# Two hybrid layers: gate and merge as one stage, the post norm by chunk, scale vectors loaded ahead

## The chip, the core and the metric

The kernel runs on one core of one Trainium2 chip. TensorE does the matrix products and the 128x128 turns (transposes), VectorE, ScalarE and GpSimd the elementwise work, SyncE (SP) issues most transfers. The metric is the device time of one execution in microseconds (us), the median of several.

## The reference, cut to what matters

The reference computes two transformer blocks with mixers and experts, and behind them two hybrid layers. The change lies in the hybrid layers alone:

```python
def hybrid_layer(x, p_i, ...):
    h = rmsnorm(x, g_pre)
    proj = h @ w_in                       # four mixers' inputs, gate paths, 4 x 1024 merge logits
    o = stack([o_a, o_b, o_c, o_d])       # sparse attention, short conv, stick-breaking attention, spatial gating
    o = o * silu(gate_paths)
    z = einsum('bsnw,nwd->bsnd', o, w_branch)
    g = sigmoid(merge_logits + b_merge)
    merged = sum(g * z, axis=2)
    y = merged @ w_out
    x = x + rmsnorm(y, g_post)
    x = x + (p_i @ w_ple) * sigmoid(x @ w_ple_gate)
    return x
```

There are 512 tokens of width 1024, everything in float32. `rmsnorm(x, g)` is `x * rsqrt(mean(x*x) + 1e-6) * g`.

## The kernel before, in words

The program is a list of stages. Each stage has one function for each engine, and the functions write out, in order, what that engine issues; nothing reorders it. A wait stands for a semaphore value, and `fence(P, e, stage)` waits until all four compute engines have reached the end of a stage. The 512 tokens are four chunks `c` of 128 rows. The eight PSUM banks are handed out in turn, and a bank is taken again when its last content has been read. Weights pass through a ring of four 2 MB slots; SP fetches the next weights as soon as the slot's user has freed it, in one fixed order.

A hybrid layer has the stages `h_norm`, `h_mix`, `h_attend`, `h_gate`, `h_merge` and `h_out`, and in `hybrid` they follow each other twice (l = 0 and 1). What each does:

- `h_norm` squares each chunk on ScalarE, forms the reciprocal root for two chunks at a time on GpSimd (`pool_rstd`: a multiply-add and a power), multiplies on VectorE with the scale vector `gpre` (a broadcast DMA that GpSimd issues), and turns h on TensorE.
- `h_gate` multiplies o by silu on VectorE and turns it into oT: TensorE turns half a chunk into a bank, and VectorE (half 0) or ScalarE (half 1) copies it out.
- `h_merge` computes the merge logits in two fp32r parts. `hp` holds hT split into a high and a low part, `wp` the same for a half (`part(p)`) of the weights: ScalarE writes the high part, VectorE three quarters of the low part and GpSimd the last quarter. There are eight quarters q of two halves each; for each q, TensorE does 2 x 96 instructions into four banks, and then four branch products (`c,oT`), one for each chunk. `place` on VectorE and ScalarE handles one chunk: add the bias, sigmoid, times the branch product, sum. The tile of the gate, `sg`, has two buffers, so the chunks take turns.
- `h_out` turns the merged rows mg, multiplies by w_out (`kept('wo')`, two column halves n of four chunks c, each copied out by ScalarE), multiplies p by w_ple, normalizes y (`norm_act` on ScalarE, `pool_rstd` on GpSimd, two instructions a chunk on VectorE), turns the new x, and multiplies by w_ple_gate.

In the profile a helper's line stands for all of its users: L62 is a product, L66 a turn, L72 an activation, L75, L81, L87 are VectorE's or GpSimd's two-input, three-input and copy instructions, L78 a multiply-add, L117 a DMA. So the names of the tiles tell the stages apart: `wp,hp` is the merge's product, `c,oT` a branch or output product, `ident,mg`, `ident,mx` and `ident,h` are the turns of the merged rows, of x (`mx`) and of h.

Of the kernel before, what the change touches and what calls it, by code (L numbers as in the profile page):

```python
# [11 lines left out]
ACT = mybir.ActivationFunctionType  # L12
# [2910 lines left out]
def hybrid(P, I, x, cs, dst, ring, front, ready):  # L2923
    for l in range(2):
        k_ = lambda *a, l=l: (f'h{l}',) + a
        with ExitStack() as c:
            oT = P.sb([128, 8, 512], name="oT", ctx=c)
            hT = P.sb([128, 8, 512], name="hT", ctx=c)
            h_norm(P, I, l, k_, x, hT, front, ready)
            with ExitStack() as d:  # L2930
                o = P.sb([128, 4, D], name="o", ctx=d)
                aV = P.sb([128, 4, 256], name="aV", ctx=d)
                qkT = P.sb([128, 4, 512], name="qkT", ctx=d)
                iT = P.sb([128, 2, 512], name="iT", ctx=d)
                big = P.sb([128, 10, 512], name="big", ctx=d)
                fc = P.sb([128, 4, 512], name="fc", ctx=d)
                tok = P.sb([128, 4, 768], name="tok", ctx=d)
                madd = x[:, 4:6].rearrange("p a (b n) -> p (a b) n", b=2)
                h_mix(P, I, l, k_, ring, cs, hT, o, aV, qkT, iT, big, fc, tok, madd)
                silu = h_attend(P, I, l, k_, ring, hT, oT, o, aV, qkT, big, fc, tok, madd)  # L2940
                h_gate(P, k_, o, oT, silu)
            mg = P.sb([128, 4, D], name="mg", ctx=c)
            h_merge(P, I, l, k_, ring, hT, oT, mg, x[:, 4:6])
            h_out(P, I, l, k_, ring, oT, mg, hT, x)
        front = k_('out')
        ready = lambda c, k_=k_: P.dve.at(*k_('xout', 4 + c))
    h_store(P, dst, x, front, ready)
# [46 lines left out]
def h_norm(P, I, l, k_, x, hT, front, ready):  # L2994
# [3 lines left out]
    g = P.sb([128, D], name="gpre", ctx=d)  # L2998
# [27 lines left out]
    def dve(e):  # L3026
        fence(P, e, front)
        e.wait_ge(*s_g.at(*k_('g')))
        for c in G4:
            e.wait_ge(*P.pool.at(*k_('rs', c // 2)))  # L3030
            e.scalar_tensor_tensor(out=h[:, c, :], in0=x[:, c, :], scalar=rs[:, c:c + 1], in1=g[:], op0=MUL, op1=MUL).then_inc(*P.dve.inc(*k_('normed', c)))
# [550 lines left out]
def h_gate(P, k_, o, oT, silu):  # L3582
    def pe(e):
        fence(P, e, k_('attend'))
        for c in G4:
            for half in range(2):
                e.wait_ge(*P.dve.at(*k_('gated', half, c)))
                pe_turns(P, e, k_('oT', c, half), [o[:, c, (4 * half + j) * 128:(4 * half + j + 1) * 128] for j in range(4)],
                         (P.act if half else P.dve,) + k_('oT', c, half))
        P.end(k_('gate'), P.pe)  # L3590

    def dst(c, half):
        return oT[:, half * 4:half * 4 + 4, c * 128:(c + 1) * 128], P.bank(*k_('oT', c, half)).rearrange("p (j n) -> p j n", j=4)

    def act(e):
        fence(P, e, k_('attend'))
        for c in G4:
            e.wait_ge(*P.pe.at(*k_('oT', c, 1)))
            e.activation(*dst(c, 1), ACT.Copy).then_inc(*P.act.inc(*k_('oT', c, 1)))
        P.end(k_('gate'), P.act)  # L3600

    def dve(e):
        fence(P, e, k_('attend'))

        def gate(c):
            for n in range(2):
                ov = o[:, c, n * 512:n * 512 + 512]
                e.scalar_tensor_tensor(out=ov, in0=ov, scalar=0.5, in1=silu[:, 2 * c + n], op0=MUL, op1=MUL).then_inc(*P.dve.inc(*k_('gated', n, c)))

        gate(0)  # L3610
        for c in G4:
            if c < 3:
                gate(c + 1)
            e.wait_ge(*P.pe.at(*k_('oT', c, 0)))
            e.tensor_copy(*dst(c, 0)).then_inc(*P.dve.inc(*k_('oT', c, 0)))
        P.end(k_('gate'), P.dve)

    def pool(e):
        fence(P, e, k_('attend'))
        P.end(k_('gate'), P.pool)  # L3620

    P.stage(pe, act, dve, pool, nothing)


def h_merge(P, I, l, k_, ring, hT, oT, mg, spare):
    d = ExitStack()
    sg, bm = (spare[:, i].rearrange("p (a n) -> p a n", a=2) for i in range(2))
# [11 lines left out]
    def in_order(part, half, place):  # L3639
        part(0)  # L3640
# [11 lines left out]

    def pe(e):
        fence(P, e, k_('gate'))
# [23 lines left out]
        def place(n, q, i):  # L3678
# [13 lines left out]
    def act(e):  # L3692
        fence(P, e, k_('gate'))
        for h in range(2):
            e.activation(hp[:, 0, 4 * h:4 * h + 4], hT[:, 4 * h:4 * h + 4], ACT.Copy).then_inc(*P.act.inc(*k_('hhigh', h)))

# [6 lines left out]
        def place(n, q, i):  # L3703
            e.wait_ge(*P.dve.at(*k_('biased', n)))
            e.activation(sg[:, n % 2, :], sg[:, n % 2, :], ACT.Sigmoid).then_inc(*P.act.inc(*k_('sig', n)))

        in_order(part, skip, place)
        P.end(k_('merge'), P.act)

    def dve(e):  # L3710
        fence(P, e, k_('gate'))
        for h in range(2):
# [7 lines left out]
        def place(n, q, i):  # L3720
            S, mv = sg[:, n % 2, :], mg[:, i, (q % 2) * 512:(q % 2) * 512 + 512]
# [14 lines left out]

        in_order(part, skip, place)
        P.end(k_('merge'), P.dve)

    def pool(e):  # L3740
        fence(P, e, k_('gate'))
# [11 lines left out]

        in_order(part, half, skip)
# [13 lines left out]
def h_out(P, I, l, k_, ring, mT, y, xT, x):  # L3768
# [38 lines left out]
    def act(e):  # L3807
# [19 lines left out]
        norm_act(P, e, k_('post'), y, junk[:], ss, G4)  # L3827
# [10 lines left out]
    def dve(e):  # L3838
# [25 lines left out]
    def pool(e):  # L3864
# [3 lines left out]
        e.wait_ge(*P.act.at(k_('post'), 'square', 3))  # L3868
        pool_rstd(P, e, rs[:, 0:4], ss[:, 0:4], D, EPS, *k_('post'))
# [28 lines left out]
def program(nc, I, out):  # L3898
    with ExitStack() as ctx:
# [20 lines left out]
        with ExitStack() as c:  # L3920
            ring = Ring(P, 4, "c", c)
            hybrid(P, I, x, cs, out[0], ring, ('moe1', 'experts'), lambda c: P.dve.at('moe1', 'result', c))
# [28 lines left out]
```

## Time and profile before

| what | value |
|---|---|
| time, median of 3 runs | 4548.87 us (4538.51 to 4552.62) |
| the profiled execution's own time | 4555.35 us |
| its span | 4553.6 us |
| mean granted TensorE clock | 0.915 |
| TensorE busy | 4006.0 us, 88% |
| VectorE, ScalarE, GpSimd busy | 1662.4, 1133.3, 414.7 us |

Busy time is summed over the span; TensorE's clock is given as a share of 2.4 GHz, and 0.5 of it is 1.2 GHz. The hybrid layers take the stretch from about 3102 us to the end. Layer 0 has its merge at 3435 to 3671 us and layer 1 at 4156 to 4391 us.

### The profile page before, as it was taken

What the parts mean: (1) busy time and instruction counts of PE and PEld (TensorE: products, weight loads), DVE (VectorE), ACT (ScalarE), POOL (GpSimd) and SP (SyncE); (2) the same over time, 40 slices, a digit from 0 to 9 for tenths busy, and PEclk for the clock granted to TensorE, in tenths of its full rate; (3) what the DMA queues carried; (4) which work ended last, traced back from release to release, by engine and by line L of the source; (5) the groups of instructions that cost most, each with busy time, mean ns of one, the idle gap of its engine ahead of it and who ended that gap; (6) DMA issues with size and microseconds to landing.
All of it is one profiled execution on the core that took longest, in us unless ns stands there. A gap on an engine that the chain in (4) does not pass through costs nothing.

```text
span 4553.6 us, 58245 instructions
## 1 busy us (share of the span) xinstructions
PE 4006.0 (88%) x25387; PEld 2336.4 (51%) x25387; DVE 1662.4 (37%) x2920; ACT 1133.3 (25%) x2163; POOL 414.7 (9%) x430
## 2 busy tenths in 40 slices
PE   7998888999999966468999798888988988988997
PEld 4546645333335424368898432224556744455753
DVE  2205531122233027755544412224643313644322
ACT  2114411111123137633343110001142211133211
POOL 2200020000000012301001100000002200001200
PEclk9999998999999977656797899999999999989999
DMA  6341034988873139733341399994103212112221
GB/s 233 111 146 33 17 121 159 370 324 326 327 274 132 43 110 297 232 111 103 91 124 50 153 384 409 409 409 180 46 1 135 99 63 79 39 37 93 102 83 37
DMA packets 358670, 739.05 MB, mean 162 GB/s; under 512 B 67184, under 2 KB 143456, under 8 KB 358416
## 3 DMA queue, kind: packets, MB, share of 16 engines
q1 hardware_dynamic: 348416, 697.93, 42.2%
q0 software_dynamic: 10000, 37.41, 2.3%
q8 instruction: 199, 3.26, 0.3%
q14 instruction: 55, 0.45, 0.0%
HBM read 673.39 MB, written 61.89 MB: 161 GB/s over the span
## 4 chain that ended last, share of the span: by engine, by line
PE 75%; DMA 9%; DVE 9%; ACT 5%; issue 1%; SPq 1%; POOL 0%; DVEq 0%; POOLq 0%; ACTq 0%
PE ps L62 72%; DMA raw<-in_moe_w_dram 6%; PE ps L66 3%; DVE mx L75 1%; ACT naS L72 1%; DMA b<-in_ada_w_dram 1%; SPq L117 1%; DVE nast L90 1%; DVE o L75 1%; DMA a<-in_ada_w_dram 0%; DVE ps L75 0%; ACT b L72 0%; ACT c L72 0%; DVE b L75 0%; DVE spr L75 0%
## 5 line engine op out<-in xcount | busy, mean ns | idle before, releaser
L62 PE MATMUL ps<-raw,xinT 128*64 128x512 f32 (+1 forms) x4096 | 595.9, 493 | 54.1 <-DMA raw<-in_moe_w_dram 45.4
L62 PE MATMUL ps<-c,hT 128*128 128x512 f32 (+2 forms) x1024 | 420.6, 565 | 5.7 <-ACT hT L72 3.5
L62 PEld LDWEIGHTS ps<-raw,xinT 128*64 128x64 f32 (+1 forms) x4096 | 194.5, 123 | 436.0 <-issue 286.2
L62 PE MATMUL ps<-wp,hp 128*128 128x512 f32 x1536 | 360.3, 396 | 20.2 <-DVE wp L75 20.2
L62 PE MATMUL ps<-a,nahT 128*128 128x512 f32 x768 | 338.2, 597 | 5.6 <-ACT nahT L72 5.2
L62 PEld LDWEIGHTS ps<-wp,hp 128*128 128x128 f32 x1536 | 290.9, 190 | 87.0 <-issue 27.0
L62 PEld LDWEIGHTS ps<-c,hT 128*128 128x128 f32 x1024 | 192.6, 193 | 201.0 <-issue 194.2
L62 PE MATMUL ps<-raw,hidT 128*64 128x512 f32 x1024 | 240.0, 604 | 16.5 <-DMA raw<-in_moe_w_dram 16.2
L62 PEld LDWEIGHTS ps<-a,nahT 128*128 128x128 f32 x768 | 144.2, 191 | 178.6 <-issue 178.0
L62 PE MATMUL ps<-c,oT 128*128 128x512 f32 x512 | 222.8, 593 | 1.4 <-ACT oT L72 1.4
L75 DVE TENSOR_TENSOR mx<-mx,ps 128x512 f32<-128x512 f32 (+1 forms) x164 | 106.6, 661 | 219.5 <-PE ps L62 184.7
L62 PEld LDWEIGHTS ps<-c,oT 128*128 128x128 f32 x512 | 97.0, 190 | 116.9 <-issue 111.0
L62 PE MATMUL ps<-xr,b 128*128 128x512 f32 (+1 forms) x384 | 143.9, 535 | 7.6 <-DVE xr L81 7.5
L62 PEld LDWEIGHTS ps<-raw,hidT 128*64 128x64 f32 x1024 | 67.2, 137 | 148.6 <-issue 113.5
L62 PE MATMUL ps<-hT,c 128*128 128x512 f32 x320 | 142.5, 606 | 0.0
L75 DVE TENSOR_TENSOR wp<-c,wp 128x1536 fp32r<-128x1536 f32 x32 | 60.4, 1892 | 221.6 <-ACT wp L72 221.6
L72 ACT ACTIVATE hidT<-ps 128x512 f32<-128x512 f32 x32 | 19.1, 597 | 453.4 <-PE ps L66 453.4
L75 DVE TENSOR_TENSOR hid<-hid,ps 128x512 f32<-128x512 f32 x64 | 44.0, 687 | 240.6 <-ACT hid L72 217.6
L75 POOL TENSOR_TENSOR wp<-c,wp 128x512 fp32r<-128x512 f32 x32 | 89.1, 2786 | 353.5 <-ACT wp L72 353.5
L81 DVE SCALAR_TENSOR_TENSOR xr<-xx,pv,xr 128x768 f32<-128x768 f32 x48 | 45.7, 1015 | 206.1 <-ACT xr L72 205.8
L72 ACT ACTIVATE wp<-c 128x2048 fp32r<-128x2048 f32 x32 | 60.9, 1910 | 217.0 <-PE ps L62 217.0
L62 PEld LDWEIGHTS ps<-xr,b 128*128 128x128 f32 x384 | 73.5, 194 | 77.4 <-issue 61.9
(456 smaller groups left out, 5866.8 us busy)
## 6 DMA issues: line engine op xcount, KB each, us to landing
raw<-in_moe_w_dram SPq DMA_DIRECT2D x384, 1024.0 KB, 9.6
c<-in_w_in_dram SPq DMA_DIRECT2D x28, 2048.0 KB, 9.1
a<-in_ada_w_dram SPq DMA_DIRECT2D x16, 2048.0 KB, 12.9
b<-in_ada_w_dram SPq DMA_DIRECT2D x8, 2048.0 KB, 10.5
a<-in_na_w_qkv_dram SPq DMA_DIRECT2D x6, 2048.0 KB, 19.0
c<-in_w_branch_dram SPq DMA_DIRECT2D x16, 512.0 KB, 4.2
c<-in_w_out_dram SPq DMA_DIRECT2D x4, 2048.0 KB, 9.1
c<-in_w_ple_gate_dram SPq DMA_DIRECT2D x4, 2048.0 KB, 7.8
```

What stands on the lines that cost most here:

```text
L62: return self.e.matmul(out, lhsT, rhs, start=start, stop=stop, skip_group_check=True) if self.e is not None else self
L66: return self.e.transpose(out, in_, ident[0:k, 0:k]) if self.e is not None else self
L72: return self.e.activation(*a, **k) if self.e is not None else self
L75: return self.e.tensor_tensor(*a, **k) if self.e is not None else self
L81: return self.e.scalar_tensor_tensor(**k) if self.e is not None else self
L90: return self.e.tensor_reduce(*a, **k) if self.e is not None else self
L117: return self.e.dma_start(*a) if self.e is not None else self
```

## The change

- `h_gate` and `h_merge` become one stage, so one fence falls away. In it ScalarE's order is: split half of hT, high part of the first weights, one turned tile, the other half of hT, three turned tiles. The first split (`low(0)`), the first low part and the second split follow VectorE's gate work.
- The gate tile `sg` has four buffers, one for each chunk, in the spare part of x (`x[:, 4:6]`), and the bias `bm` has a tile of its own. VectorE adds the bias for all four chunks of a quarter first, then does the rest chunk by chunk.
- In `h_out` the square of chunk c is issued right behind the copy of y's second half for that chunk, inside `kept('wo')`, and the reciprocal root is formed for each chunk.
- In `h_norm` the scale vector lies in `x[:, 4]`, and its load is issued behind the merge stage (layer 1) or behind the routing of the second expert stage (layer 0). The reciprocal root is formed for each chunk.

On ScalarE, at the start of the merge of layer 0 (`hp` is hT split, `wp<-c` the high part of weights, `oT<-ps` a turned tile copied out):

```order
 L72 ACTIVATE o<-ps 128x256 x2
-L72 ACTIVATE oT<-ps 128x4x128 x4
-L72 ACTIVATE hp<-hT 128x2048 x2
-L72 ACTIVATE wp<-c 128x2048 x4
+L72 ACTIVATE hp<-hT 128x2048
+L72 ACTIVATE wp<-c 128x2048
+L72 ACTIVATE oT<-ps 128x4x128
+L72 ACTIVATE hp<-hT 128x2048
+L72 ACTIVATE oT<-ps 128x4x128 x3
+L72 ACTIVATE wp<-c 128x2048 x3
 L72 ACT_TABLE_LOAD
```

The splits of hT and the first high part moved ahead of the turned tiles; the number of instructions is the same.

On ScalarE, in the output stage of layer 0 (`mg<-ps` is a copy of y, `ojunk,oss` a square with its sum, `pT` and `ple` the tiles of p):

```order
-L72 ACTIVATE mg<-ps 128x512 x8
+L72 ACTIVATE mg<-ps 128x512 x5
+L72 ACTIVATE ojunk,oss<-mg 128x1024
+L72 ACTIVATE mg<-ps 128x512
+L72 ACTIVATE ojunk,oss<-mg 128x1024
+L72 ACTIVATE mg<-ps 128x512
+L72 ACTIVATE ojunk,oss<-mg 128x1024
+L72 ACTIVATE mg<-ps 128x512
+L72 ACTIVATE ojunk,oss<-mg 128x1024
 L72 ACTIVATE pT<-ps 128x512 x2
 L72 ACTIVATE ple<-ps 128x512 x8
-L72 ACTIVATE ojunk,oss<-mg 128x1024 x4
```

The four squares moved from behind the ple copies to between the copies of y, and the last of them stands ahead of the two copies of pT.

On VectorE, in the last quarter of the merge of layer 0, before (`mx` is the gate tile, `mg` the merged rows):

```order
L75 TENSOR_TENSOR mx<-ps,mx 128x512
L75 TENSOR_TENSOR mx<-mx,ps 128x512
L75 TENSOR_TENSOR mg<-mg,mx 128x512
L75 TENSOR_TENSOR mx<-ps,mx 128x512
L75 TENSOR_TENSOR mx<-mx,ps 128x512
L75 TENSOR_TENSOR mg<-mg,mx 128x512
L87 COPY oT<-ps 128x4x128 x4
```

and now:

```order
L75 TENSOR_TENSOR mx<-ps,bm 128x512 x4
L75 TENSOR_TENSOR mx<-mx,ps 128x512
L75 TENSOR_TENSOR mg<-mg,mx 128x512
L75 TENSOR_TENSOR mx<-mx,ps 128x512
L75 TENSOR_TENSOR mg<-mg,mx 128x512
L75 TENSOR_TENSOR mx<-mx,ps 128x512
L75 TENSOR_TENSOR mg<-mg,mx 128x512
L75 TENSOR_TENSOR mx<-mx,ps 128x512
L75 TENSOR_TENSOR mg<-mg,mx 128x512
L87 COPY oT<-ps 128x4x128 x4
```

The first excerpt shows the last two of four chunks; the adds of all four now stand together at the front.

The diff, cut to its core:

```diff
@@ h_norm
-    g = P.sb([128, D], name="gpre", ctx=d)
+    g = x[:, 4, :]
...
+        fence(P, e, spare)
+        e.dma_start(g, bc(I['g_pre_2'][l])).then_inc(*s_g.inc(*k_('g')))
         fence(P, e, front)
-        e.dma_start(g[:], bc(I['g_pre_2'][l])).then_inc(*s_g.inc(*k_('g')))
-        for i in range(2):
-            e.wait_ge(*P.act.at(k_('norm'), 'square', 2 * i + 1))
-            pool_rstd(P, e, rs[:, 2 * i:2 * i + 2], ss[:, 2 * i:2 * i + 2], D, EPS, *k_('rs', i))
+        for c in G4:
+            e.wait_ge(*P.act.at(k_('norm'), 'square', c))
+            pool_rstd(P, e, rs[:, c:c + 1], ss[:, c:c + 1], D, EPS, *k_('rs', c))
@@ h_merge, ScalarE
-        fence(P, e, k_('gate'))
-        for h in range(2):
+        fence(P, e, k_('attend'))
+        def high(h):
             e.activation(hp[:, 0, 4 * h:4 * h + 4], hT[:, 4 * h:4 * h + 4], ACT.Copy).then_inc(*P.act.inc(*k_('hhigh', h)))
...
+        high(0)
+        part(0)
+        turn(0)
+        high(1)
+        for c in (1, 2, 3):
+            turn(c)
         in_order(part, skip, place)
@@ h_merge, VectorE
-            e.wait_ge(*P.pe.at(*k_('merge', 2 * q + 1, i, 'half')))
-            e.wait_ge(*s_b[q % 2].at(*k_('bm', q)))
-            if n >= 2:
-                e.wait_ge(*P.dve.at(*k_('merged', n - 2)))
-            e.tensor_tensor(S, P.bank(*k_('merge', q, i)), bm[:, q % 2, :], ADD).then_inc(*P.dve.inc(*k_('biased', n)))
+            for j in G4 if i == 0 else ():
+                e.wait_ge(*P.pe.at(*k_('merge', 2 * q + 1, j, 'half')))
+                e.wait_ge(*s_b[q % 2].at(*k_('bm', q)))
+                if q:
+                    e.wait_ge(*P.dve.at(*k_('merged', n + j - 4)))
+                e.tensor_tensor(sg[:, j, :], P.bank(*k_('merge', q, j)), bm[:, q % 2, :], ADD).then_inc(*P.dve.inc(*k_('biased', n + j)))
+            if n == 0:
+                e.wait_ge(*P.pe.at(*k_('oT', 3, 1)))
...
+        gate(0)
+        for c in G4:
+            if c < 3:
+                gate(c + 1)
+            e.wait_ge(*P.pe.at(*k_('oT', c, 0)))
+            e.tensor_copy(*turned(c, 0)).then_inc(*P.dve.inc(*k_('oT', c, 0)))
+        low(0)
+        part(0)
+        low(1)
         in_order(part, skip, place)
@@ h_out
+                    if what == 'wo' and n == 1:
+                        e.wait_ge(*P.act.last())
+                        e.activation(junk[:], y[:, c, :], ACT.Square, accum_out=ss[:, c:c + 1]).then_inc(*P.act.inc(*k_('post', 'square', c)))
...
-        norm_act(P, e, k_('post'), y, junk[:], ss, G4)
...
-        e.wait_ge(*P.act.at(k_('post'), 'square', 3))
-        pool_rstd(P, e, rs[:, 0:4], ss[:, 0:4], D, EPS, *k_('post'))
+        for c in G4:
+            e.wait_ge(*P.act.at(*k_('post', 'square', c)))
+            pool_rstd(P, e, rs[:, c:c + 1], ss[:, c:c + 1], D, EPS, *k_('post', c))
```

## Rows read from the trace of the kernel before

**Rows 1.** The page: the span, and TensorE's busy time.
```profile
span 4553.6 us, 58245 instructions
...
PE 4006.0 (88%) x25387; PEld 2336.4 (51%) x25387; DVE 1662.4 (37%) x2920; ACT 1133.3 (25%) x2163; POOL 414.7 (9%) x430
```

**Rows 2.** Waits, 3380 us on: who waited for whom; us in total, times, longest.
```profile
PE ps L66 <- DVE mx L75: 21.9, 8, 9.5
...
PE ps L62 <- DVE wp L75: 20.2, 2, 10.1
...
PE ps L66 <- DVE h L81: 9.7, 1, 9.7
...
PE ps L66 <- DVE mg L75: 9.6, 2, 4.8
```

**Rows 3.** Chain of waits through layer 0: start us, us, what.
```profile
3425.86 1.92 ACT hp L72
...
3427.91 4.49 DVE hp L75 x2
3432.40 2.76 DVE wp L75
...
3435.29 226.02 PE ps L62 x884
```

**Rows 4.** DMA issues, 3418.3 to 3419 us: KB each, us to landing.
```profile
c<-in_w_in_dram SPq DMA_DIRECT2D x1, 2048.0 KB, 8.9
```

**Rows 5.** Timeline, start of merge: start, us, engine, line, what [idle before <-releaser].
```profile
3418.32 0.37 SPq L117 DMA_DIRECT2D c<-in_w_in_dram  x1
...
3450.27 1.76 DVE L75 TENSOR_TENSOR wp<-c,wp 128x1536 fp32r<-128x1536 f32 x1 [12.38 <-ACT wp L72]
3450.33 2.85 POOL L75 TENSOR_TENSOR wp<-c,wp 128x512 fp32r<-128x512 f32 x1 [13.48 <-ACT wp L72]
```

**Rows 6.** Timeline, last quarter of layer 0's merge.
```profile
3659.42 7.03 PE L62 MATMUL ps<-c,oT 128*128 128x512 f32 x16
...
3661.34 0.69 DVE L75 TENSOR_TENSOR mx<-mx,ps 128x512 f32<-128x512 f32 x1 [9.19 <-PE ps L62]
...
3663.39 0.63 ACT L72 ACTIVATE mx<-mx 128x512 f32<-128x512 f32 x1 [10.57 <-DVE mx L75]
...
3670.40 0.69 DVE L75 TENSOR_TENSOR mg<-mg,mx 128x512 f32<-128x512 f32 x1
```

**Rows 7.** Timeline, output stage of layer 0.
```profile
3732.31 1.04 PE L66 MATMUL ps<-ident,pp 128*128 128x128 f32 x8
...
3734.14 14.00 PE L62 MATMUL ps<-c,pT 128*128 128x512 f32 x32 [0.79 <-ACT pT L72]
...
3748.80 1.06 ACT L72 ACTIVATE ojunk<-mg 128x1024 f32<-128x1024 f32 x1
...
3767.64 7.56 PE L62 MATMUL ps<-c,hT 128*128 128x512 f32 x17 [0.69 <-ACT hT L72]
```

**Rows 8.** Windows, turns of mg and x: us, busy (count), PEclk, DMA share, GB/s.
```profile
3671.20:3677.20 6.00, 5.34 (x32) 5.14 (x32) 2.77 (x4) 2.37 (x4) 1.30 (x2) 0.72 0.55 175
3757.60:3767.20 9.60, 7.87 (x32) 6.28 (x32) 9.50 (x10) 2.00 (x4) 0.00 (x0) 0.52 0.00 0
```

**Rows 9.** Timeline, norm of layer 1.
```profile
3823.54 10.51 SPq L117 DMA_DIRECT2D c<-in_w_in_dram  x4
...
3831.11 4.87 DVE L81 SCALAR_TENSOR_TENSOR h<-mx,hrs,gpre 128x1024 f32<-128x1024 f32 x4 [6.19 <-DMA gpre<-in_g_pre_dram]
...
3839.86 2.38 PE L62 MATMUL ps<-c,hT 128*128 128x512 f32 x5 [0.73 <-ACT hT L72]
```

**Rows 10.** Timeline, norm of layer 0: VectorE's first pair, GpSimd's second power.
```profile
3109.68 2.48 DVE L81 SCALAR_TENSOR_TENSOR h<-mx,hrs,gpre 128x1024 f32<-128x1024 f32 x2
...
3111.10 1.62 POOL L75 TENSOR_TENSOR hrs<-hrs,mhalf 128x2 f32<-128x2 f32 x1
```

**Rows 11.** Tile hrs: GpSimd's powers in the norms; ns min/median/max.
```profile
L75 POOL TENSOR_TENSOR hrs<-hrs,mhalf x4: 688/726/1620, 3108.0 to 3828.7; 128x2 f32<-128x2 f32 x4
```

More of the change, by code:

```diff
@@ L2920, with hybrid @@
 G4 = range(4)
-def hybrid(P, I, x, cs, dst, ring, front, ready):
+def hybrid(P, I, x, cs, dst, ring, front, spare, ready):
     for l in range(2):
@@ L2940, in hybrid @@
                 silu = h_attend(P, I, l, k_, ring, hT, oT, o, aV, qkT, big, fc, tok, madd)
[L2941 removed]
             mg = P.sb([128, 4, D], name="mg", ctx=c)
[L2943 removed]
+            h_merge(P, I, l, k_, ring, hT, o, oT, silu, mg, x[:, 4:6])
             h_out(P, I, l, k_, ring, oT, mg, hT, x)
[L2945 removed]
+        front, spare = k_('out'), k_('merge')
         ready = lambda c, k_=k_: P.dve.at(*k_('xout', 4 + c))
@@ L3579, in h_attend, with h_merge @@
     return silu
[L3582 to L3625, printed above, removed]
+def h_merge(P, I, l, k_, ring, hT, o, oT, silu, mg, spare):
     d = ExitStack()
-    sg, bm = (spare[:, i].rearrange("p (a n) -> p a n", a=2) for i in range(2))
+    sg = spare.rearrange("p a (b n) -> p (a b) n", b=2)
+    bm = P.sb([128, 2, 512], name="bm", ctx=d)
     hp = P.sb([128, 2, 8, 512], F32R, name="hp", ctx=d)
@@ L3651, in skip, with turned @@
         pass
+    def turned(c, half):
+        return oT[:, half * 4:half * 4 + 4, c * 128:(c + 1) * 128], P.bank(*k_('oT', c, half)).rearrange("p (j n) -> p j n", j=4)
     def pe(e):
-        fence(P, e, k_('gate'))
+        fence(P, e, k_('attend'))
+        for c in G4:
+            for half in range(2):
+                e.wait_ge(*P.dve.at(*k_('gated', half, c)))
+                pe_turns(P, e, k_('oT', c, half), [o[:, c, (4 * half + j) * 128:(4 * half + j + 1) * 128] for j in range(4)],
+                         (P.act if half else P.dve,) + k_('oT', c, half))
         def half(q, h):
@@ L3692, in act, with turn @@
     def act(e):
-        fence(P, e, k_('gate'))
-        for h in range(2):
+        fence(P, e, k_('attend'))
+        def high(h):
             e.activation(hp[:, 0, 4 * h:4 * h + 4], hT[:, 4 * h:4 * h + 4], ACT.Copy).then_inc(*P.act.inc(*k_('hhigh', h)))
+        def turn(c):
+            e.wait_ge(*P.pe.at(*k_('oT', c, 1)))
+            e.activation(*turned(c, 1), ACT.Copy).then_inc(*P.act.inc(*k_('oT', c, 1)))
         def part(p):
@@ L3710, in dve, with gate, low @@
     def dve(e):
-        fence(P, e, k_('gate'))
-        for h in range(2):
+        fence(P, e, k_('attend'))
+        def gate(c):
+            for n in range(2):
+                ov = o[:, c, n * 512:n * 512 + 512]
+                e.scalar_tensor_tensor(out=ov, in0=ov, scalar=0.5, in1=silu[:, 2 * c + n], op0=MUL, op1=MUL).then_inc(*P.dve.inc(*k_('gated', n, c)))
+        def low(h):
             e.wait_ge(*P.act.at(*k_('hhigh', h)))
@@ L3740, in pool @@
     def pool(e):
-        fence(P, e, k_('gate'))
+        fence(P, e, k_('attend'))
         def part(p):
@@ L3752, in half @@
                 e.dma_start(bm[:, q % 2, :], bc(I['b_merge_2'][l, c0:c0 + 512])).then_inc(*s_b[q % 2].inc(*k_('bm', q)))
+        part(0)
         in_order(part, half, skip)
@@ L3921, in program @@
             ring = Ring(P, 4, "c", c)
-            hybrid(P, I, x, cs, out[0], ring, ('moe1', 'experts'), lambda c: P.dve.at('moe1', 'result', c))
+            hybrid(P, I, x, cs, out[0], ring, ('moe1', 'experts'), ('moe1', 'route'), lambda c: P.dve.at('moe1', 'result', c))
         P.emit()
```

19 lines of the change are left out of this document (11 added, 8 removed).

## The prediction

> **What bounds the kernel now.** I read the page first, then the table of waits of the hybrid layers (the stretch from 3380 us on), then the chain of waits through layer 0 of them, and last the timelines around every hole in TensorE's row. TensorE is busy for 88% of the span [rows 1]; a change that touches no matmul can only win the holes in its row. In the hybrid layers the table of waits names four of them that the diff touches: before the merge's first product (10.1 us, twice), before the turns of the merged rows (4.8, twice), before the turns of the new x (9.5 and three times 0.5, twice), and before the turns of the normed rows of layer 1 (9.7, once) [rows 2]. Inside the eight quarters of a merge TensorE never waits: the chain has one piece of 226 us of products there [rows 3]. So what the diff does inside a quarter is worth nothing as long as that stays so, and the forecast is what becomes of the four holes.
>
> The sum is made against the profiled execution (4555.35 us, span 4553.6); the median of the three timed runs, 4548.87, lies 6.5 below it and the gain is taken off that. Times below are places in the profile of before, layer 0; layer 1 repeats them. From no change this measurement can tell about 0.3%, 13.6 us.
>
> **A. Start of the merge.** Now ScalarE finishes the last turned tile at 3425.8, splits hT in two pieces until 3429.6, VectorE answers with 4.49 us for the low halves and 2.76 for the first weights' low part, and TensorE starts at 3435.29 [rows 3]. The change issues the same instructions, earlier: ScalarE's first split of hT can start when attention ends (3418.4) and VectorE's `low(0)` follows its last gate copy at 3425.7, at 2.25 (half of 4.49), so to 3427.95. ScalarE's next instruction, `part(0)`, waits for the weights. Their transfer is issued at 3418.32, when attention frees the ring's slot, and lands 8.9 us later [rows 4, 5]: 3427.2. The change doesn't move that. Queued behind this wait on ScalarE are `turn(0)`, the second split of hT, `turn(1)` to `turn(3)` and `part(1)`; TensorE's turns don't wait for them, since eight turned tiles fill eight banks. So: 3427.3 + 1.92 (ScalarE, as for the equally wide split of hT) = 3429.2, + 1.76 on VectorE [rows 5] + waits = 3431.1, TensorE at 3431.2 instead of 3435.3. Its second half, wanted 12 us later, gets `high(1)` at 3435.3 and its low part at 3437.2, in time. The clock falls in both cases: TensorE's turns end at 3425.2 (10.09 before its start [rows 2]) and 6.0 us of idleness are left, where 4.8 us were followed by turns at half clock (below). I take **4.1 a layer, 8.2**. Bounds: no gain if those weights land 4 us later; at most 4.3, since they can't be used before they land.
>
> For VectorE's 1.76: in the steady quarters VectorE and GpSimd start together on their shares of a part, VectorE 0.06 earlier, with 1.76 and 2.85 us [rows 5]; in the first one of before, GpSimd was ahead and VectorE needed 2.76 [rows 3]. In the new order both wait for the same ScalarE instruction, so I take 1.76. The other order would cost 1.0 a layer.
>
> **B. End of the merge.** In the last quarter VectorE waits 9.19 us for the first branch product, then does bias add, (ScalarE's sigmoid,) product, sum for each tile in turn; the last product of TensorE ends at 3666.45 and VectorE's last sum only at 3671.1 [rows 6]. With four gate tiles the four adds and sigmoids are done before the first branch product is there: the fourth half product ends at 3659.4, its add (0.69) and sigmoid (0.63) by 3661.0. What is left behind a branch product is a product and a sum, 1.4 us, less than the 1.76 between two branch products (7.03 for four). The last ends at 3666.6 + 1.4 = 3668.0, and the turns start at 3668.15 instead of 3671.24: 3.1 us. The turns themselves take 5.34 us at a mean clock of 0.72 [rows 8], where eight warm ones take 1.04, so 32 take 4.2 [rows 7]; with 1.7 us of idleness in place of 4.8 the clock may hold. I take half of that 1.1: **3.6 a layer, 7.2** (bounds 3.1 and 4.2).
>
> **C. Post norm.** Now the four squares (1.06 us, one each 1.18) follow the copies of the ple product, then GpSimd's scale, then VectorE's two instructions a chunk pace the turns, and TensorE, done at 3748.14, starts the gate product at 3767.64 [rows 7]. In the change the square of chunk c follows its second copy. TensorE takes 0.44 us for an instruction (14.00 for 32 [rows 7]) and 16 of them for such a chunk, 7.0, so squares 0 to 2, their scales and the updates of x lie beside the output product. Square 3 stands ahead of the two copies of pT on ScalarE, which TensorE waits for: the ple product starts 1.3 us later (1.18 and the wait for the copy) and ends at 3749.4. From the last square (3753.5 now) to the first turn (3757.6) it is 4.1 today, so the fourth square, done at 3734.4, has its update by 3738.5: 11 us early. The turns run at once: 4.2 warm [rows 7] and 0.7 for the last copy, gate product at 3754.3. Gain **13.3 a layer, 26.6**. If the turns stay at half clock (7.87 for 32 [rows 8]), it is 9.6.
>
> **D. Norm of layer 1.** Now VectorE waits 6.2 us for the scale vector, which GpSimd issues only when layer 0 is over; it starts at 3831.1, and the projections start at 3839.86 [rows 9]. Preloaded, into a part of x that the merge leaves free, it is long there: its issue stands behind scale 3 at 3736, on an idle GpSimd. Next in line is GpSimd's scale of each chunk, and here the row of layer 0 speaks: with VectorE in its normalizing instruction GpSimd's power took 1.62 us where the median of four is 0.73, and ended 0.56 after VectorE's second instruction did [rows 10, 11]. Four single scales now alternate with four instructions of 1.28 (4.87 for four, overlapped). The first starts at about 3826.0 (layer 0's end, 3823.54, a square of 1.18, GpSimd's 0.3 + 0.73, waits), then each chunk 1.28 + 0.56 + 0.1 later, the last starting at about 3831.9 and done at 3833.2; four copies of 0.62 follow, projections at 3835.9. Gain **3.9**. The first weights, issued at 3823.54 [rows 9] at the same event as now, land at 3832.5 by the 8.9 of [rows 4], and so don't bound it; they are the upper bound, 7.3. Without that blocking: h done at 3830.9, start at 3833.7, gain 6.2.
>
> The Trainium skill (SBUF — State Buffer, "Who interferes with whom") has the rule for it: a Vector instruction with two SBUF inputs and a GpSimd one that reads SBUF exclude each other, and the second waits for the whole of the first. The trace agrees with 1.62 against 0.73. It speaks against splitting the scale by chunk; by the rule the sum is as here, without it 4500.
>
> **E. Norm of layer 0.** There the scale vector was in time already. VectorE's four instructions came in two pairs; with single scales the third and the fourth each wait: the fourth starts at about 3114.7 instead of 3114.0. **Loss 0.8** (between a loss of 1.5 and a gain of 0.6, if scale 3 slips in ahead).
>
> Sum: 8.2 + 7.2 + 26.6 + 3.9 - 0.8 = 45.1, so 4510.3 for a profiled execution and 4503.8 for the median.
>
> **At no cost.** The gate stage's fence goes; its work starts at the same moment. `bm` in a tile of its own changes an address. Inside a quarter VectorE now does four adds, then four products (and sums), 12 x 0.69 = 8.3 us; TensorE's products of the next quarter want only its adds, which come earlier than now. ScalarE's functions keep their order of kinds, so no table is loaded more. More small instructions on GpSimd lie in its idle time, but for D and E. The matmuls are the same in number and order.
>
> **Rivals.**
> R1, no blocking in the norms (D 6.2, E a gain of 0.6): 4500. Against it stands the 1.62.
> R2, the cheap end: the clock stays low over the turns (C 9.6, B 3.1) and the merge's first weights land too late for A: 0 + 6.2 + 19.2 + 3.9 - 0.8 = 28.5, 4520. For it: turns of x at clock 0.52 [rows 8]; against it: they followed 9.5 us of idleness that goes.
> R3, the change doesn't do what it says: the time comes back as waits for weights, since SP's loads start with fences that the change doesn't move. It needs landings 3 us (D) or, for the first half of w_ple_gate, tens of us later than now; no change, 4540 to 4549.
> R4, slower: the quarters lose their cover. VectorE's block of 8.3 us begins only when its parts are done and holds up the next parts, on which TensorE's halves wait. Now the next part can't start before TensorE has finished the half after (11.2 us into the next quarter, 18 after the branches begin), while the block ends 12 after they begin, and a part is wanted 6 us after it can be done: 12 us a quarter before the first is lost. From 4.2 us lost in each of 14 quarters the kernel is slower by over 0.3%; at 4.5 it would be at 4567. The single piece of 226 us [rows 3] speaks against.
>
> **How the numbers follow.** Forecast 0.67, R1 0.13, R2 0.13, R3 0.05, R4 0.02. The three first are faster by over 0.3%: 0.93; same 0.05; slower 0.02. Range: all terms at their best give 4498, at their worst 4522; the three runs of before lie 14 us apart, so the lower end goes 12 further: 4486 to 4522.
>
> **What would show it.** Merge: TensorE idle 6.0 before its first half, with ScalarE's `part(0)` ended by the DMA; 1.7 before the mg turns. Out: no idleness between ple product and turns, turns of x in 4.2 to 5.3, pT's wait 2.1. Layer 1 norm: no DMA wait, GpSimd's powers at 1.1 to 1.7 us, and 13 us in all from gate product to projections. Wrong is the forecast if a quarter takes more than 28.64 us, or if ScalarE's wait for weights lasts past 3429.

## The result and the profile after

| what | before | after |
|---|---|---|
| median of four runs on one chip | 4550.74 us (4538.51 to 4560.48) | 4498.98 us (4494.41 to 4503.99) |
| the profiled execution's own time | 4555.35 us | 4494.41 us |
| its span | 4553.6 us | 4492.6 us |
| mean granted clock | 0.915 | 0.923 |

The ratio of the times is 0.9888, with a 95% interval of 0.9860 to 0.9915: faster by 51.8 us; the interval reaches from 38.7 to 63.7 us, so the times alone don't tell the forecast of 45.1 from rival R1 (48.8), and the rows below have to. The page of the kernel after, against [rows 1]:

```profile
span 4492.6 us, 58286 instructions
PE 3980.7 (89%) x25387; PEld 2313.7 (52%) x25387; DVE 1655.2 (37%) x2920; ACT 1131.0 (25%) x2163; POOL 428.0 (10%) x450
```

TensorE has the same 25387 instructions. The two profiled spans lie 61.0 us apart, and 9.2 of them have nothing to do with the change: the last product ahead of the hybrid layers (`hl`) ends at 3108.71 us before and at 3099.48 after, in code that is the same but for the early load of layer 0's scale vector (in the kernels of this study it ends anywhere from 3084.95 to 3108.71). So every comparison below starts at that product and ends at the start of the last gate product (`w_ple_gate`). That stretch fell from 1379.16 to 1327.37 us, by 51.8. That this is the timed difference too is chance: it holds 2.7 us of stretches that the change doesn't touch. Cut at TensorE's own instructions it divides like this (us, layer 0 and layer 1):

| stretch on TensorE | before | after |
|---|---|---|
| norm of layer 0, to the projections | 9.14 | 10.00 |
| projections, mixers and attention (not touched) | 307.35 / 305.67 | 305.04 / 305.31 |
| idle before the merge's first half | 10.09 / 10.09 | 5.78 / 5.70 |
| the first half | 23.65 / 23.60 | 24.04 / 24.06 |
| from its end to the last branch product | 207.51 / 207.51 | 207.50 / 207.50 |
| wait and turns of the merged rows | 10.82 / 10.79 | 5.97 / 5.97 |
| output product to gate product | 90.37 / 90.35 | 76.22 / 76.22 |
| gate product of layer 0 and norm of layer 1 | 72.22 | 68.06 |

The waits of the stretch from 3090 us on, next to [rows 2] (columns: us in all, times, longest):

```profile
PE ps L62 <- DVE wp L75: 11.5, 2, 5.8
ACT wp L72 <- DMA c<-in_w_in_dram: 13.9, 2, 7.0
PE ps L66 <- DVE h L81: 7.1, 5, 4.4
```

The hole before the merge is 5.8 us instead of 10.1. The row of the DMA says what bounds it now: ScalarE stands 7.0 us, twice, before the first weights. The waits for `mx`, which were the largest item, are gone.

Start of the merge of layer 0, timeline (columns: start, us, engine, line, operation; in brackets the idle time before it and what ended it), against [rows 3 to 5]:

```profile
3407.64 0.37 SPq L117 DMA_DIRECT2D c<-in_w_in_dram  x1
...
3407.65 1.92 ACT L72 ACTIVATE hp<-hT 128x2048 fp32r<-128x2048 f32 x1
...
3414.92 2.28 DVE L75 TENSOR_TENSOR hp<-hT,hp 128x2048 fp32r<-128x2048 f32 x1
...
3416.55 1.91 ACT L72 ACTIVATE wp<-c 128x2048 fp32r<-128x2048 f32 x1 [6.99 <-DMA c<-in_w_in_dram]
...
3418.49 1.76 DVE L75 TENSOR_TENSOR wp<-c,wp 128x1536 fp32r<-128x1536 f32 x1 [1.29 <-ACT wp L72]
...
3420.30 24.19 PE L62 MATMUL ps<-wp,hp 128*128 128x512 f32 x96 [5.79 <-DVE wp L75]
```

The weights are asked for at 3407.64 and are there at 3416.5, 8.9 later; then 1.91 on ScalarE and 1.76 on VectorE follow one another with hardly a gap, and TensorE starts. This is the forecast chain, with the forecast durations.

End of the merge, against [rows 6]:

```profile
3645.02 0.69 DVE L75 TENSOR_TENSOR mx<-ps,bm 128x512 f32<-128x512 f32 x1 [2.03 <-PE ps L62]
...
3646.73 0.69 DVE L75 TENSOR_TENSOR mx<-mx,ps 128x512 f32<-128x512 f32 x1 [1.02 <-PE ps L62]
...
3652.61 0.69 DVE L75 TENSOR_TENSOR mg<-mg,mx 128x512 f32<-128x512 f32 x1
3653.44 3.69 PE L66 MATMUL ps<-ident,mg 128*128 128x128 f32 x32 [1.60 <-DVE mg L75]
```

VectorE's last sum ends at 3653.30, and TensorE has waited 1.60 instead of 4.79. Its 32 turns take 3.69 instead of 5.34, and the window over them shows a granted clock of 1.00, where [rows 8] had 0.72 (columns: stretch and its length, busy us and instructions of PE, PEld, DVE, ACT, POOL, then the granted clock, DMA share, GB/s):

```profile
3420.30:3444.30 24.00, 24.00 (x96) 19.67 (x97) 6.28 (x3) 5.62 (x6) 7.38 (x4) 0.91 0.46 152
3653.40:3657.10 3.70, 3.66 (x32) 3.48 (x32) 2.45 (x4) 1.79 (x3) 1.30 (x2) 1.00 0.79 226
3729.70:3733.40 3.70, 3.65 (x33) 3.41 (x31) 2.53 (x4) 2.41 (x5) 0.00 (x0) 1.00 0.00 0
```

The first row is the merge's first half, behind its 5.8 us of idleness and still partly at half clock (1.2 GHz; mean 0.91); the second is the turns of the merged rows, the third those of the new x, which had 0.52 in [rows 8]. In the output stage, against [rows 7]:

```profile
3713.68 1.06 ACT L72 ACTIVATE ojunk<-mg 128x1024 f32<-128x1024 f32 x1
3714.74 1.06 ACT L72 ACTIVATE pT<-ps 128x512 f32<-128x512 f32 x2
3715.85 14.00 PE L62 MATMUL ps<-c,pT 128*128 128x512 f32 x32 [1.97 <-ACT pT L72]
...
3717.09 1.23 DVE L75 TENSOR_TENSOR mx<-mx,mg 128x1024 f32<-128x1024 f32 x1
...
3729.69 3.66 PE L66 MATMUL ps<-ident,mx 128*128 128x128 f32 x32
...
3734.03 3.27 PE L62 MATMUL ps<-c,hT 128*128 128x512 f32 x7 [0.69 <-ACT hT L72]
```

The fourth square ends ahead of pT's copies, the last update of x starts at 3717.09, and the turns at 3729.69 follow the ple product with no bracket, which means with no wait.

Norm of layer 1, against [rows 9]:

```profile
3791.25 0.18 POOL L78 TENSOR_SCALAR hrs<-hss 128x1 f32<-128x1 f32 x1 [74.95 <-ACT hjunk L72]
...
3792.20 1.28 DVE L81 SCALAR_TENSOR_TENSOR h<-mx,hrs 128x1024 f32<-128x1024 f32 x1 [0.88 <-POOL hrs L75]
3792.32 1.22 POOL L78 TENSOR_SCALAR hrs<-hss 128x1 f32<-128x1 f32 x1 [0.25 <-ACT hjunk L72]
...
3794.20 1.28 DVE L81 SCALAR_TENSOR_TENSOR h<-mx,hrs 128x1024 f32<-128x1024 f32 x1 [0.72 <-POOL hrs L75]
3794.25 1.28 POOL L78 TENSOR_SCALAR hrs<-hss 128x1 f32<-128x1 f32 x1
3795.62 0.55 POOL L75 TENSOR_TENSOR hrs<-hrs,mhalf 128x1 f32<-128x1 f32 x1
```

No DMA ends a wait here any more. A new one stands in its place: VectorE and GpSimd alternate. GpSimd's multiply-add on 128 numbers takes 0.18 alone and 1.22 to 1.28 where VectorE has started its 1.28 us instruction just ahead of it, and VectorE then waits 0.72 for the scale of the next chunk. VectorE's instructions start 2.0 apart; the four took 4.87 in one piece before. From the end of the gate product to the projections it is 12.9 us, where the prediction named 13.

### The profile page after: what moved, and what is told of

Its sections match the earlier page's. It is cut to its first block, busy times and chain, and to the rows that moved or that the text cites. A ratio compares the mean times of both kernels' runs of the same rounds, so it can differ in the third digit from the quotient of the medians.

```text
span 4492.6 us, 58286 instructions
## 1 busy us (share of the span) xinstructions
PE 3980.7 (89%) x25387; PEld 2313.7 (52%) x25387; DVE 1655.2 (37%) x2920; ACT 1131.0 (25%) x2163; POOL 428.0 (10%) x450
## 4 chain that ended last, share of the span: by engine, by line
PE 75%; DMA 10%; DVE 8%; ACT 4%; issue 1%; SPq 1%; POOL 1%; POOLq 0%; DVEq 0%; ACTq 0%
PE ps L62 73%; DMA raw<-in_moe_w_dram 6%; PE ps L66 2%; DMA b<-in_ada_w_dram 1%; DVE mx L75 1%; ACT naS L72 1%; SPq L117 1%; DVE nast L90 1%; DVE o L75 1%; DMA a<-in_ada_w_dram 0%; DVE ps L75 0%; DVE spr L75 0%; DMA c<-in_w_in_dram 0%; ACT b L72 0%; DVE b L75 0%
```

## The experiments

All start from the kernel after. Where a single profiled execution is told, the stretches above are compared, not the whole times, since the parts ahead of the hybrid layers differ by up to 24 us between executions of the same code. All but `u_post`, `combo` and `again` have one execution only, and their rows are single samples. How far a row scatters is told where it matters.

**Are the early splits the gain at the start?** The order of the splits and turned tiles is put back; the fence stays out and the four gate tiles stay.

```diff
-        high(0); part(0); turn(0); high(1)
-        for c in (1, 2, 3): turn(c)
+        for c in G4: turn(c)
+        high(0); high(1); part(0)
...
-        low(0); part(0); low(1)
+        low(0); low(1); part(0)
```

> The changed kernel, but in the merge stage ScalarE first copies its four turned tiles, then splits hT twice, then takes the first weights, and VectorE does both low halves of hT before the first low part: the old order inside the new stage. My theory (the early splits are what shortens the hole before the merge's first product, and the fused stage by itself gives nothing): TensorE's wait before the first wp,hp product goes from 5.8 back to 10.1 us in both layers, the first half runs in 23.8 instead of 24.2, all else stays, so about 4 us a layer. Rival (the removed fence is what pays): the wait stays near 5.8.

The hole is 9.75 us in both layers and the first half 23.66 and 23.68: 3.6 of the 3.9 us a layer come back.

```profile
3431.67 8.63 PE L62 MATMUL ps<-wp,hp 128*128 128x512 f32 x29 [9.75 <-DVE wp L75]
```

The order of the splits is the cause. The 0.3 us a layer that stay are too small to be given to the parts that were left in: in the nine kernels of this study with the new order, hole and first half together take 29.66 to 30.06 us.

**Are four gate tiles the gain at the end?** Two tiles again, and the chunks take turns.

```diff
-            S = sg[:, i, :]
-            for j in G4 if i == 0 else ():  ... add the bias of chunk j
+            S = sg[:, n % 2, :]
+            if n >= 2: e.wait_ge(*P.dve.at(*k_('merged', n - 2)))
+            ... add the bias of chunk i
```

> The changed kernel with two gate buffers again and the bias add of a chunk next to its product. Theory: the wait before the turns of mg goes from 1.6 back to 4.8 us and the 32 turns from 3.69 to 5.3, because the longer idleness lets TensorE's clock fall: 4.8 us a layer. Rival: the turns are short for another reason (the place of the stage), so they stay at 3.7 and only 3.2 us a layer come back. Inside the quarters nothing: 28.64 us each.

```profile
3642.16 5.35 PE L66 MATMUL ps<-ident,mg 128*128 128x128 f32 x32 [4.79 <-DVE mg L75]
```

```profile
3642.20:3647.50 5.30, 5.30 (x32) 5.07 (x32) 2.47 (x4) 1.79 (x3) 1.30 (x2) 0.68 0.63 191
3647.60:3706.20 58.60, 56.07 (x136) 25.19 (x136) 7.77 (x8) 10.88 (x19) 3.05 (x9) 1.00 0.13 44
3706.30:3721.90 15.60, 15.60 (x34) 6.77 (x35) 2.36 (x2) 4.18 (x7) 0.38 (x1) 0.89 0.37 141
```

The wait is 4.79 again and the turns 5.35 at a clock of 0.68: 4.85 us a layer, the whole term. So 3.19 of it is the wait, and 1.66 is the clock, which 4.8 us of idleness in front lowered and 1.6 us did not. The third window was foreseen by no theory: the ple product took 15.70 instead of 14.00 with a clock of 0.89 in its stretch, 1.7 us more in each layer, although nothing had waited longer there (1.96). The kernel before had the same 4.79 us ahead of the turns but 0.79 ahead of the ple product, and 14.00 for it; the kernel after has 1.60 and 1.97, and 14.00. Only `u_tail` has both waits long. So two of the changed kernel's parts are not independent: with B alone undone, 13.1 us come back, 9.7 at the end of the merge and 3.4 here. The whole time of this single execution, 4493.26, is below that of the kernel after and says nothing: its parts ahead of the hybrid layers were 12.5 us shorter.

**Does the post norm by chunk pay, and which part of it?** In `u_post` the four squares go behind the ple copies again and there is one scale for four chunks; in `p_once` the squares stay early and only the scale is formed once.

```diff
 both
-        for c in G4:
-            e.wait_ge(*P.act.at(k_('post', 'square', c)))
-            pool_rstd(P, e, rs[:, c:c + 1], ss[:, c:c + 1], D, EPS, *k_('post', c))
+        e.wait_ge(*P.act.at(k_('post', 'square', 3)))
+        pool_rstd(P, e, rs[:, 0:4], ss[:, 0:4], D, EPS, *k_('post'))
 u_post also
-                    if what == 'wo' and n == 1:  ... square of chunk c
...
+        kept('ple', ple)
+        for c in G4:  ... square of chunk c
```

> The changed kernel with the post norm as before: four squares behind the ple copies, one reciprocal root for four. Theory: from the first output product to the first gate product 90.4 instead of 76.2 us, 28.3 us for both layers, so some 0.6% of the time: about 4527. Rival (the updates of x beside the output product slow TensorE or ScalarE there, so that part of the gain is given back in the changed kernel): under 26 us come back.

> The changed kernel with the squares at their new place, but one reciprocal root for all four chunks, behind the fourth square, and the updates of x behind it. Theory: the four updates (2.46 us each) end about 12 us after the fourth square, still before the ple product's 14 us are over, so the chunkwise scale in the output stage is worth nothing: 0 us, turns of x start without a wait. Rival (the scale by chunk carries part of the gain): the turns of x wait, 2 us or more a layer.

`u_post` took 4526.48 us (median of 6, ratio to before 0.9958, interval 0.9941 to 0.9975): 27.5 above the kernel after as first timed, 28.9 above it as timed again below. In its profile the output stage is 90.4 and 90.2 us again, and 2.0 more are lost behind it:

```profile
3730.93 1.97 PE L66 MATMUL ps<-ident,mx 128*128 128x128 f32 x8 [9.48 <-DVE mx L75]
...
3740.95 57.22 PE L62 MATMUL ps<-c,hT 128*128 128x512 f32 x128 [0.69 <-ACT hT L72]
```

```profile
3740.95:3745.95 5.00, 5.00 (x7) 2.23 (x8) 0.00 (x0) 0.00 (x0) 0.00 (x0) 0.59 0.00 0
3745.95:3798.00 52.05, 52.05 (x122) 22.80 (x120) 9.69 (x14) 4.18 (x7) 0.00 (x0) 1.00 0.00 0
```

The 9.48 us of idleness lower the clock for the turns and, here, for the first 5 us of the gate product too (57.22 instead of 55.20; layer 1's, behind the stretch compared here, takes 57.47). The kernel before had 9.49 us of idleness at the same place and 55.20 for the product, so this part doesn't come each time. `p_once` left the output stage at 76.22 in both layers, and its span is that of the kernel after, 4492.6: the position of the squares does all of it, and the scale by chunk does nothing there, since 11 us of cover lie over it.

**Is the preload the gain in layer 1's norm, and what does the split by chunk cost?** `u_pre` issues the scale vector behind the fence of the layer before, as before; `n_pairs` keeps the preload and forms the scale for two chunks at a time in `h_norm`.

```diff
 u_pre
-        fence(P, e, spare)
-        e.dma_start(g, ...)
         fence(P, e, front)
+        e.dma_start(g, ...)
 n_pairs
-        for c in G4:
-            e.wait_ge(*P.act.at(k_('norm'), 'square', c))
-            pool_rstd(P, e, rs[:, c:c + 1], ...)
+        for i in range(2):
+            e.wait_ge(*P.act.at(k_('norm'), 'square', 2 * i + 1))
+            pool_rstd(P, e, rs[:, 2 * i:2 * i + 2], ...)
```

> The changed kernel with the load of the norm's scale vector issued behind the end of the stage before, as before, but with the scales by chunk. Theory: layer 1's norm waits for the transfer again (about 6 us on VectorE) and from the first gate product to the projections it takes 72 us instead of 68.1; since all four scales are then there, VectorE's four instructions run without a pause. Layer 0: within 0.3 us of now. Rival (the preload is not needed once the scales come one by one): under 1 us.

> The changed kernel with the reciprocal roots of the norm formed for two chunks at a time, as before, and the preload kept. Theory (GpSimd's multiply-add is held up by the VectorE instruction that runs beside it, so each single scale costs a pause of 0.7 us): layer 0's norm gets its 0.85 us back (from the end of the last expert product to the projections 9.15 instead of 10.0), layer 1's is equal within 0.5 us. Rival (singles are as good or better in both): layer 0 doesn't gain, layer 1 loses 1 us or more.

In `u_pre` the wait for the DMA is back, 6.29, and the stretch from gate product to projections is 71.61 instead of 68.06: the preload is worth 3.55 us. VectorE's four instructions, all scales being ready by then, run in one piece:

```profile
3803.44 4.87 DVE L81 SCALAR_TENSOR_TENSOR h<-mx,hrs 128x1024 f32<-128x1024 f32 x4 [6.29 <-DMA mx<-in_g_pre_dram]
```

In `n_pairs` it is 67.89, 0.17 less, and layer 0's norm is 9.81 where 9.15 was expected of it. That was a miss, and the rows show why (layer 0):

```profile
3101.98 1.29 POOL L78 TENSOR_SCALAR hrs<-hss 128x2 f32<-128x2 f32 x1 [1.38 <-ACT hjunk L72]
...
3104.09 2.48 DVE L81 SCALAR_TENSOR_TENSOR h<-mx,hrs 128x1024 f32<-128x1024 f32 x2 [0.88 <-POOL hrs L75]
```

The pair's multiply-add was held up as well, for 1.29, and VectorE paused 0.88 once. Pairs don't avoid the blocking; they meet it once instead of up to three times. Nor is 9.81 a size to rely on: `combo` below, with the same code in layer 0's norm, has 9.20.

**Is it the two SBUF inputs?** VectorE's normalizing instruction takes its second input from two PSUM banks in place of the scale vector, so this kernel leaves the norm's scale vector out; nothing else changes.

```diff
-            e.scalar_tensor_tensor(out=h[:, c, :], in0=x[:, c, :], scalar=rs[:, c:c + 1], in1=g, ...)
+            e.scalar_tensor_tensor(out=..., in0=..., scalar=rs[:, c:c + 1], in1=P.psum[:, b0:b0 + 2, :], ...)
```

> The changed kernel, but in the norms VectorE multiplies by what lies in two PSUM banks instead of by the scale vector (this leaves the scale vector out and so changes the values; instructions, sizes and order are the same). VectorE's instruction then has one input in SBUF. Theory (two inputs in SBUF on VectorE shut out a GpSimd instruction that reads SBUF): GpSimd's multiply-adds of 1.28 us become 0.19, VectorE's four instructions follow each other without a pause of 0.72, layer 1's norm is 2.1 us shorter (66.0 instead of 68.1 from gate product to projections), layer 0's 1.1. Rival (GpSimd is slow there because of the transfers of weights running at the same time, or of its waits): the multiply-adds stay at 1.2 to 1.3.

```profile
3105.50 4.85 DVE L81 SCALAR_TENSOR_TENSOR h<-mx,hrs,ps 128x1024 f32<-128x1024 f32 x4
...
3105.70 0.19 POOL L78 TENSOR_SCALAR hrs<-hss 128x1 f32<-128x1 f32 x1 [0.41 <-ACT hjunk L72]
...
3106.94 0.19 POOL L78 TENSOR_SCALAR hrs<-hss 128x1 f32<-128x1 f32 x1 [0.41 <-ACT hjunk L72]
```

The same multiply-adds, beside the same long VectorE instructions, take 0.19; the four instructions stand in a row; layer 1 gains 2.43 us and layer 0 1.37. That is the blocking of the prediction, and against this one execution of the kernel after it costs 3.8 us in all. Layer 1's part is firm, for gate product and norm take 68.05 to 68.07 in the kernel after and in six others with this norm; layer 0's is not, as its norm scatters from 8.78 to 10.45 with the same code, against 8.63 here. The Trainium skill (SBUF — State Buffer, "Who interferes with whom") says that a Vector instruction with at most one SBUF input, outside the modes that use both port pairs, does not contend with GpSimd. The trace agrees, with 0.19 against 1.28.

**Can the weights come earlier at the merge?** Each load of the ring has a number, and the number gives its slot. In `s_slot` the merge stage first passes over two numbers, so its first two loads go to slots that are free much earlier: the first weights are asked for at 3366.11, 46 us before attention ends. The two lines hold the releases of the two slots that are passed over (attention's last read, VectorE's last gate product), for the loads that take them later.

```diff
+    ring.load(lent_done)
+    ring.load((P.dve,) + k_('gated', 1, 3))
     for q in range(8):
```

> The changed kernel with the ring's numbering shifted by two in the merge stage: the first merge weights go to a slot that has been free since the middle of attention, instead of the one that attention's last unit frees; the number of transfers is the same. Theory (the hole before the merge is bound by the landing of these weights, and behind it by VectorE's queue: gates and copies until 7.3 us after attention's end, then 2.24 and 1.76): ScalarE's wait for the transfer goes, and TensorE's wait is 4.6 instead of 5.8 us. Rival A (ScalarE's queue behind the weights is the bound): it falls to 3 or less. Rival B (the landing isn't the bound): 5.8 stays.

```profile
3416.41 1.60 POOL L75 TENSOR_TENSOR wp<-c,wp 128x512 fp32r<-128x512 f32 x1 [11.35 <-DVE o L81]
...
3417.40 1.77 DVE L81 SCALAR_TENSOR_TENSOR o<-o,c 128x512 f32<-128x512 f32 x2
...
3422.39 1.29 POOL L75 TENSOR_TENSOR wp<-c,wp 128x512 fp32r<-128x512 f32 x1 [4.37 <-ACT wp L72]
3422.49 2.81 DVE L75 TENSOR_TENSOR wp<-c,wp 128x1536 fp32r<-128x1536 f32 x1
3425.35 24.01 PE L62 MATMUL ps<-wp,hp 128*128 128x512 f32 x96 [5.47 <-DVE wp L75]
```

ScalarE's wait for the DMA is gone, yet the hole is 5.47 us, not the 4.6 that were expected. The chain now runs over VectorE's gate work, and GpSimd, early now, gets in its way: two gate instructions take 1.77 instead of 1.28, and in front of the low part GpSimd's share starts 0.10 ahead of VectorE's, which then takes 2.81 instead of 1.76. Of the 1.2 us a layer that were expected, 0.2 to 0.3 came against the kernel after; but its two holes (5.79 and 5.71) are among the shortest, since in the nine kernels with the same code they range from 5.71 to 6.27, with a mean of 5.98, and against that it is 0.5. From 5.47 to the 4.6 that were expected 0.87 is missing, and the 1.05 by which VectorE's instruction is longer cover it.

**Can pT's copies go ahead of the fourth square?**

```diff
+                        if c == 3:
+                            for i in range(2):  ... copy pT, half i
                         ... square of chunk c
```

> The changed kernel with the two copies of pT ahead of the fourth square on ScalarE. Theory: TensorE's wait before the ple product goes from 1.97 to about 0.9 us, the fourth update of x is 1 us later and still hidden, so 1.1 us a layer are won. Rival (the square's place doesn't matter, the wait is the copies' own): no change.

```profile
3705.85 14.00 PE L62 MATMUL ps<-c,pT 128*128 128x512 f32 x32 [0.79 <-ACT pT L72]
```

The wait before the ple product is 0.79 instead of 1.97 and the output stage 75.04 instead of 76.22, in both layers. Nothing behind it comes later.

**All together, and the kernel after once more.** `combo` has the edits of `s_slot`, `p_pT` and `n_pairs`; `again` is the kernel after, unchanged.

> The changed kernel with three edits that go together: the first merge weights in the slot that is free earlier, pT's copies ahead of the fourth square, norm scales in pairs with the preload kept. Theory: 2 x 1.2 + 2 x 1.1 + about 1 = 5.6 us less than the changed kernel, 4493; against before 0.9875. Rival: each hides behind another bound, and no difference is seen.

> The changed kernel once more, on the same chip as the version with three more edits, as its yardstick. Expected 0.989 of before, 4499 us.

| kernel | median of 6 runs | ratio to before | interval | hybrid stretch |
|---|---|---|---|---|
| again | 4497.57 us | 0.9901 | 0.9882 to 0.9921 | 1327.71 us |
| combo | 4490.71 us | 0.9877 | 0.9856 to 0.9897 | 1321.13 us |

The stretch is 6.6 us shorter, 2.1 of it in projections, mixers and attention, which have the same code in both, and 0.8 in layer 0's norm, which scatters. The median is 6.9 shorter, but the intervals overlap: `combo` is faster than before for certain, while against the kernel after the times alone don't settle it. The rows do for two of its parts: idle 5.47 and 0.79 where the kernel after has 5.7 to 6.3 and 1.97. `again` is 49.5 us below before (4547.03 in that series of runs): a second timing of the change, 2.3 us less than the first.

## Why the prediction was right

The forecast was 4503.8 and the kernel took 4498.98. The mechanisms of A, B and C held, and that of D at another instruction than was named; the turns in B and C were mis-sized, and the size of E is partly luck. By its terms, both layers together:

| term | forecast | measured | undone alone |
|---|---|---|---|
| A, start of the merge | 8.2 | 7.9 | 7.3 |
| B, end of the merge | 7.2 | 9.7 | 9.7 |
| C, post norm | 26.6 | 28.3 | 28.1 |
| D, norm of layer 1 | 3.9 | 4.2 | 3.6 |
| E, norm of layer 0 | -0.8 | -0.9 | -0.2 (`n_pairs`), -0.8 (`combo`) |
| stretches not touched | 0 | 2.7 | |
| sum | 45.1 | 51.8 | |

- **A** held step by step: DMA 8.9, then 1.91 and 1.76. The hole fell by 4.3 and 4.4; the first half took 0.4 more (mean clock 0.91 over it, 0.92 before). Over the nine kernels with this order the hole's mean is 5.98, the forecast's 6.0, and the gain in hole and first half 3.8 a layer, against the 4.1 that were forecast: what the first half gives back was not in the sum.
- **B** was mis-sized by 1.25 a layer. The wait fell from 4.79 to 1.60, within 0.1 of the forecast. For the turns I took half of a gain of 1.1; the clock held and the gain was 1.65, since 32 turns in a row take 3.69, not the 4.2 that four times an eighth of them would (a group of eight by itself takes 1.04, 0.12 more than eight of the long row). So even the upper bound, 4.2 a layer, was too low: the estimate of the warm turns was the part that failed.
- **C** was mis-sized by 0.85 a layer, for the same reason: mostly turns of 3.66 instead of 4.2, and the ple product delayed by 1.18 instead of 1.3. The mechanism and its condition (no half clock, rival R2) came as told. The thing the forecast gave to "by chunk" belongs to the moved squares alone (`p_once`).
- **D** has the right size, and the blocking was there, but not at the instruction that was named. The text said that GpSimd's power would be held up, at 1.1 to 1.7 us. In layer 1 it was the multiply-add ahead of it (1.22 to 1.28), and all four powers took 0.55. The pause per chunk is 0.72, and the forecast had 0.66, so the sum came out.
- **E** came out in part by luck. In layer 0 one power was held up as named (1.47) and two multiply-adds as well (1.12 and 1.28). But its norm takes 8.78 to 10.45 us in eight executions with the same code, against 9.14 before: anything from a gain of 0.4 to a loss of 1.3, with a mean loss of 0.5. The bounds of the forecast, a gain of 0.6 to a loss of 1.5, hold all of them. `n_psum`, the norms without blocking, is 3.8 us better, where rival R1 had 3.7; 1.4 of these lie in layer 0 and scatter with it.
- **At no cost**: from the end of the first half on, a merge stayed at 207.5 us, to 0.01. R4 doesn't occur, and neither does R3: of the four holes only that of A ends with a DMA, as forecast.
- **Not foreseen**: 2.7 us in stretches with unchanged code. In the kernels of this study with the same code there, layer 0's stretch of projections, mixers and attention takes 304.4 to 305.6 us, and 307.35 before; twice it was 303.4 and 303.5. The record speaks against the change as the cause. `n_psum` is a changed kernel, and its layer 1 takes 307.36 in this stretch, longer in the same rows as layer 0 of before. The first long product of the mixers (`hT,c`), in before, in `n_psum` and in the kernel after:

```profile
3175.48 29.83 PE L62 MATMUL ps<-hT,c 128*128 128x512 f32 x64
...
3859.24 29.83 PE L62 MATMUL ps<-hT,c 128*128 128x512 f32 x64
...
3166.86 28.70 PE L62 MATMUL ps<-hT,c 128*128 128x512 f32 x64
```

So the long form comes with the change too, and what it is worth by the rows is 49.1 us, 51.8 less these 2.7; the second timing, `again`, has 49.5. Why one execution gets the long form and another not, no run tells.

The experiments that put one edit back lose 7.3, 9.7, 28.1 and 3.6 us in its own stretch, 48.6 in all (the sums here are made from unrounded numbers); with E's loss and the 2.7 of the untouched stretches this makes 50.5 of the 51.8. The 3.4 us that `u_tail` loses in its ple products are not in it. In its profile `u_post` loses 31.2 us up to the last gate product, 2.0 of them in layer 0's gate product; the timed difference is 27.5 to 28.9, and whether all executions have those 2.0 the single profile doesn't tell.

## What to carry to other kernels

A hole in TensorE's row costs its length and can cost a lowered clock behind it, so size it together with the turns or products that follow: 4.8 us of idleness cost 1.7 more, 9.5 us cost 4.2 more in the turns behind them (7.87 against 3.66), and 1.6 us cost nothing more. Look for work that a queue holds behind something it doesn't need: two reorderings (squares on ScalarE, splits on ScalarE and VectorE) gave seven tenths of this gain without one instruction less. Before splitting a small GpSimd step so that VectorE starts sooner, look at whether VectorE's long instructions have two inputs in SBUF, since each piece can then wait for a whole one of them.

## What the runs showed of the hardware beyond the forecast

- **The blocking goes both ways, and 0.05 to 0.1 us decide.** With VectorE 0.05 ahead, GpSimd's multiply-add on 128 numbers takes 1.28 instead of 0.18; with GpSimd 0.10 ahead, VectorE's 1.76 became 2.81. So the norm of layer 0, with the same code, took from 8.78 to 10.45 us in eight profiled executions. In `p_once` GpSimd's third multiply-add started 0.07 ahead of VectorE and took 0.19, the fourth waited 0.56 only, and three of VectorE's instructions ran on:

```profile
3101.69 0.19 POOL L78 TENSOR_SCALAR hrs<-hss 128x1 f32<-128x1 f32 x1 [0.88 <-ACT hjunk L72]
...
3101.76 3.67 DVE L81 SCALAR_TENSOR_TENSOR h<-mx,hrs 128x1024 f32<-128x1024 f32 x3
...
3103.53 0.75 POOL L78 TENSOR_SCALAR hrs<-hss 128x1 f32<-128x1 f32 x1
```

- **A row of turns keeps the clock.** After the 14 us of the ple product, 32 turns ran at 1.00, and after 1.6 us of idleness the merged rows' too, at 0.115 us each; after 4.8 us the same turns had 0.68 to 0.72.
- **A lowered clock can show far behind a hole.** In `u_tail` the turns behind the 4.8 us ran at 0.68, the next 58.6 us at 1.00, and the ple product behind them, after a wait of 1.96, at 0.89. The same wait of 1.97 in the kernel after left it at 14.00 us. Whether the 4.8 us have to do with it, and how, no run here tells.
